# Hybrid decoder trunk: sums of squares in two rounded passes, forget columns as weights and rest in one block, second unit staged next to the scan

## What is computed

```python
def _rmsnorm(x, g, eps):
    return x * rsqrt(mean(x * x, axis=-1) + eps) * g
# mixer
u = _rmsnorm(h, mix_norm)
z = u @ w_in       # diff q/k/v | fox q/k/v | forget (8 columns) | stick q/k/v | gates
log_f = log_sigmoid(forget_logit + forget_bias)      # 8 heads
c = cumsum(log_f, axis=tokens)
# forgetting attention: logits[q, k] += c[q] - c[k]
```

## Time and profile before

| | us |
|---|---|
| time, median of 3 runs (2472.60 to 2472.94) | 2472.61 |
| the profiled execution, its own time | 2474.14 |
| its span, first to last instruction | 2472.4 |
| PE busy, share of the span | 99% |
| DVE busy, share of the span | 87% |
| ACT busy, share of the span | 60% |
| mean granted TensorE clock, share of the full 2.4 GHz | 0.998 |

### The profile page before, as it was taken

The page is one execution under the profiler, slowest core; times in us unless marked ns, Lnnn a source line. Parts: engine busy times, 40 slices in busy tenths (PEclk is TensorE's granted clock), DMA queues, the critical chain, the costliest instruction groups (busy, mean ns, idle before and its releaser), DMA issues.

```text
span 2472.4 us, 48558 instructions
## 1 busy us (share of the span) xinstructions
PE 2450.5 (99%) x15664; PEld 2220.4 (90%) x15664; DVE 2147.3 (87%) x3881; ACT 1471.4 (60%) x2882; POOL 4.4 (0%) x13
## 2 busy tenths in 40 slices
PE   8999999999999999999999999999999999999998
PEld 7999888888899889998889998888888998899987
DVE  8999868898898779998699997798898986799986
ACT  7666447777654456664466664577776554566643
POOL 0000000000000000000000000000000000000000
PEclk9999999999999999999999999999999999999999
DMA  4332332212232333233322223222212323233333
GB/s 159 113 105 102 111 103 62 68 61 61 76 104 85 96 102 103 102 106 119 108 95 102 102 94 128 86 69 67 62 60 69 103 103 102 87 111 109 102 111 103
DMA packets 65254, 235.57 MB, mean 95 GB/s; under 512 B 7232, under 2 KB 7616, under 8 KB 65088
## 3 DMA queue, kind: packets, MB, share of 16 engines
q1 hardware_dynamic: 65088, 233.51, 28.7%
HBM read 231.38 MB, written 2.10 MB: 94 GB/s over the span
## 4 chain that ended last, share of the span: by engine, by line
PE 90%; DVE 5%; ACT 2%; issue 2%; DMA 0%; DVEq 0%; SPq 0%; ACTq 0%
PE ps L657 28%; PE ps L659 28%; PE ps L658 28%; PE ps L829 1%; DVE w_lo L1721 1%; PE ps L818 1%; PE ps L872 1%; PE ps L871 1%; PE ps L820 1%; DVE area L1721 1%; DMA w_raw<-weights 0%; PE ps L885 0%; PE ps L835 0%; PE ps L886 0%; ACT w_hi L1111 0%
## 5 line engine op out<-in xcount | busy, mean ns | idle before, releaser
L1111 ACT ACTIVATE w_hi<-w_raw 128x512 fp32r<-128x512 f32 (+1 forms) x876 | 628.3, 724 | 473.2 <-PE ps L659 230.5
L1721 DVE TENSOR_TENSOR w_lo<-w_raw,w_hi 128x512 fp32r<-128x512 f32 (+1 forms) x876 | 703.0, 808 | 116.3 <-ACT w_hi L1111 100.3
L657 PE MATMUL ps<-u_hi,w_hi 128*128 128x256 f32 (+1 forms) x2432 | 790.4, 325 | 5.1 <-DVE w_lo L1721 3.3
L659 PE MATMUL ps<-u_hi,w_lo 128*128 128x256 f32 (+1 forms) x2432 | 781.9, 322 | 0.0
L658 PE MATMUL ps<-u_lo,w_hi 128*128 128x256 f32 (+1 forms) x2432 | 781.2, 321 | 0.0
L658 PE MATMUL ps<-area,w_hi 128*128 128x256 f32 (+1 forms) x1764 | 581.4, 330 | 0.0
L657 PEld LDWEIGHTS ps<-u_hi,w_hi 128*128 128x128 f32 x2432 | 463.8, 191 | 43.6 <-issue 5.2
L659 PEld LDWEIGHTS ps<-u_hi,w_lo 128*128 128x128 f32 x2432 | 463.6, 191 | 35.0
L658 PEld LDWEIGHTS ps<-u_lo,w_hi 128*128 128x128 f32 x2432 | 464.0, 191 | 33.3 <-issue 1.4
L657 PE MATMUL ps<-area,w_hi 128*128 128x256 f32 (+1 forms) x1400 | 480.5, 343 | 0.4 <-DVE h L1743 0.4
L659 PE MATMUL ps<-area,w_lo 128*128 128x256 f32 (+1 forms) x1400 | 478.1, 341 | 0.0
(11 more groups left out here) (185 smaller groups left out, 2926.1 us busy)
## 6 DMA issues: line engine op xcount, KB each, us to landing
w_raw<-weights SPq DMA_DIRECT2D x435, 512.0 KB, 3.6
h<-x SPq DMA_DIRECT2D x4, 512.0 KB, 7.8
out<-scratch_whole SPq DMA_DIRECT2D x8, 256.0 KB, 2.2
scratch_whole<-const_b SPq DMA_DIRECT2D x1, 512.0 KB, 9.7
scratch_whole<-lambdas SPq DMA_DIRECT2D x1, 256.0 KB, 2.7
scratch_whole<-const_r SPq DMA_DIRECT2D x1, 192.0 KB, 8.9
cst<-const SPq DMA_DIRECT2D x1, 137.0 KB, 7.9
par<-params SPq DMA_DIRECT2D x1, 94.0 KB, 2.4
```

Source lines behind the costliest of these rows:

```text
L657: pe.matmul(dst, hi, x_hi, start=start, stop=False, **kw)
L659: return pe.matmul(dst, lo, x_hi, start=False, stop=stop, **kw)
L1111: return act.activation(dst, src, ACT.Copy)
L1721: return dve.tensor_tensor(dst, src, hi_part.bitcast(F32), ALU.subtract)
```

## The change

Four parts.

1. `sum_of_squares` becomes two float32r passes: ACT rounds `acc` to `acc_hi` (`squares_hi`), DVE makes `acc_lo = acc - acc_hi` (`squares_lo`), and PE multiplies each by ones. The two halves lie in piece 6 of `w_hi` and `w_lo`. The last of the seven sums stays as it was. PE now waits for `acc_lo_set`.
2. Places: `squares_lo` stands in DVE's program of an FFN after `second`, in a mixer after the `lo` of the forget blocks. `squares_hi` stands on ACT in an FFN after `scaled`, in a mixer after the `hi` of the forget blocks.
3. A forget block now holds the rounded columns in its first 64 columns and their rest in the other 64, so PE does two passes instead of three. Its result has the two parts on the two halves of the partitions: ACT copies them crosswise (two copies of 64x512 from PSUM), DVE adds them and multiplies by `rstd`.
4. DVE's `take(1)` moves from behind `bias_l` to right behind the scan, and `qk_lo(2, 2, 1)` of a mixer's first tile from behind the key bias to ahead of it.

The diff, without the lists of semaphores:

```diff
-R_IDENT, R_CAUSAL, R_STRICT, ROUNDED = 0, 1, 2, 3
+R_IDENT, R_CAUSAL, R_STRICT, R_ONES, ROUNDED = 0, 1, 2, 3, 4
+IN_BF16 = R_ONES
...
+        ones_r = sb("ones_r", P, F32R)
...
+        acc_hi, acc_lo = (w[:, (PIECES - 1) * SEQ:PIECES * SEQ] for w in (w_hi, w_lo))
...
             def sum_of_squares():
+
+                c.skip(acc_set, ND)
+                pe.wait_ge(acc_lo_set, c.next(acc_lo_set))
+                pe.matmul(ps[:, 7, :], ones_r[:], acc_hi, start=True, stop=False)
+                pe.matmul(ps[:, 7, :], ones_r[:], acc_lo, start=False, stop=True).then_inc(ms_set, 1)
+
+            def last_sum_of_squares():
 
                 pe.wait_ge(acc_set, c.next(acc_set, ND))
                 pe.matmul(ps[:, 7, :], ones, acc, start=True, stop=True).then_inc(ms_set, 1)
...
                     at = PT_HI + k * P
-                    last = three(ps[:, AUX, :], area[:, at:at + P], area[:, at + ND * P:at + ND * P + P], *u(k),
-                                 start=k == 0, stop=k == ND - 1)
+                    u_k_hi, u_k_lo = u(k)
+                    pe.matmul(ps[:, AUX, :], area[:, at:at + P], u_k_hi, start=k == 0, stop=False)
+                    last = pe.matmul(ps[:, AUX, :], area[:, at:at + P], u_k_lo, start=False, stop=k == ND - 1)
...
+            def squares_hi():
+
+                act.wait_ge(acc_set, c.next(acc_set, ND))
+                hi(acc_hi, acc).then_inc(acc_hi_set, 1)
...
                 scaled(3, own + 3)
+                squares_hi()
                 across_hi(0)
...
                 for k in range(ND):
-                    dst = wf_bank[:, k * P:(k + 1) * P].rearrange("p (r n) -> p r n", n=N_FOX)
-                    last = hi(dst, wf_source(layer, k))
+                    last = hi(wf_part(k, 0), wf_source(layer, k))
                 last.then_inc(wf_hi_set, 1)
+                squares_hi()
                 norm()
                 split(0)
                 qk_hi(2, 0, 0)
+                act.wait_ge(forget_mm, layer + 1)
+                for hd in range(2):
+                    last = act.activation(tile(4)[half(hd), :], ps[half(1 - hd), AUX, :], ACT.Copy)
+                last.then_inc(forget_turned, 1)
                 act.wait_ge(forget_in, c.next(forget_in))
...
-            hi(cst_b[:], scratch[:, 0:ROUNDED * P])
+            hi(cst_b[:], scratch[:, 0:IN_BF16 * P])
+            hi(ones_r[:], scratch[:, IN_BF16 * P:ROUNDED * P])
...
+            def squares_lo():
+
+                dve.wait_ge(acc_hi_set, c.next(acc_hi_set))
+                lo(acc_lo, acc, acc_hi).then_inc(acc_lo_set, 1)
...
                 second(3, own + 7)
+                squares_lo()
                 turned_sum(0, own)
...
-                    last = lo(dst, wf_source(layer, k), hi_part)
+                    last = lo(wf_part(k, 1), wf_source(layer, k), wf_part(k, 0))
                 last.then_inc(wf_set, 1)
+                squares_lo()
                 dve.wait_ge(rstd_set, c.next(rstd_set))
...
-                dve.tensor_tensor(y, ps[:, AUX, :], rstd[:], ALU.mult).then_inc(vec_done, 1)
+                dve.wait_ge(forget_turned, layer + 1)
+                dve.tensor_tensor(y, ps[:, AUX, :], run, ALU.add).then_inc(vec_done, 1)
+                dve.wait_ge(vec_done, c.next(vec_done))
+                dve.tensor_tensor(y, y, rstd[:], ALU.mult).then_inc(vec_done, 1)
...
                 dve.tensor_tensor_scan(run, soft, neg, 0.0, ALU.add, ALU.add).then_inc(forget_in, 1)
+                take(1, 1.0)
...
-                stage(1, 1.0)
+                split(1)
+                qk_lo(2, 2, 1)
                 dve.scalar_tensor_tensor(neg, run_hi, mask(2), base_r[:], ALU.mult, ALU.add).then_inc(vec_done, 1)
...
                     qk_lo(2, 0, 0)
-                qk_lo(2, 2, 1)
+                    qk_lo(2, 2, 1)
                 take(2, 1.0)
```

More of the change, by code:

```diff
@@ L218, in trunk @@
         cst = sb("cst", C_END)
-        cst_b = sb("cst_b", ROUNDED * P, BF16)
+        cst_b = sb("cst_b", IN_BF16 * P, BF16)
+        ones_r = sb("ones_r", P, F32R)
         par = sb("par", P_END)
@@ L453, in trunk @@
         acc_set = sem("acc_set")
+        acc_hi_set = sem("acc_hi_set")
+        acc_lo_set = sem("acc_lo_set")
         u_hi_set = sem("u_hi_set")
@@ L468, in trunk @@
         forget_mm = sem("forget_mm")
+        forget_turned = sem("forget_turned")
         forget_in = sem("forget_in")
@@ L650, in _ @@
         def _(pe):
-            c = Counts(pe, [g_part_set, snap_set, w_set, u_set, acc_set, rstd_set, hid_set, g_set, h_set, wf_set, staged,
+            c = Counts(pe, [acc_lo_set, g_part_set, snap_set, w_set, u_set, acc_set, rstd_set, hid_set, g_set, h_set, wf_set, staged,
                             rows_set, qk_set, v_set, exp_set, prob_set, pt_set, o_sq, o_rstd, o_norm,
@@ L1062, in _ @@
                 pe.matmul(ps[:, 0, :], area[:, 0:P], area[:, 0:SEQ], start=True, stop=True)
-            sum_of_squares()
+            last_sum_of_squares()
         SQ = tile(5)
@@ L1070, in times @@
             return par[:, bass.ds(gain, 1)]
-        wf_bank = area[:, PT_HI:PT_HI + 2 * ND * P]
+        wf_bank = area[:, PT_HI:PT_HI + ND * P]
         def neg_max(buf, i):
@@ L1085, in wf_source, with wf_part @@
             at = P_WF + layer * (ND * N_FOX) + k * N_FOX
-            return par[:, bass.ds(at, N_FOX)].unsqueeze(1).broadcast_to([P, P // N_FOX, N_FOX])
+            return par[:, bass.ds(at, N_FOX)].unsqueeze(1).broadcast_to([P, HEAD // N_FOX, N_FOX])
+        def wf_part(k, part):
+            at = k * P + part * HEAD
+            return wf_bank[:, at:at + HEAD].rearrange("p (r n) -> p r n", n=N_FOX)
         def keys(part, j):
@@ L1105, in _ @@
         def _(act):
-            c = Counts(act, [sum_set, *landed, unit_done, act_done, h_set, ms_set, gate_in, hid_set, forget_in,
+            c = Counts(act, [acc_set, sum_set, *landed, unit_done, act_done, h_set, ms_set, gate_in, hid_set, forget_in,
                              staged, turned, score_set, max_set, probs_turned, o_mm, o_ms,
@@ L1714, in _ @@
         def _(dve):
-            c = Counts(dve, [w_hi_set, w_set, sum_set, snap_set, unit_done, vec_done, h_set, sq_set, acc_set, u_hi_set,
+            c = Counts(dve, [acc_hi_set, w_hi_set, w_set, sum_set, snap_set, unit_done, vec_done, h_set, sq_set, acc_set, u_hi_set,
                              rstd_set, gate_out, g_hi_set, qk_hi_set,
@@ L2148, in forget @@
                 for k in range(ND):
-                    dst, hi_part = (wf_bank[:, (n + k) * P:(n + k + 1) * P].rearrange("p (r n) -> p r n", n=N_FOX)
-                                    for n in (ND, 0))
-                    last = lo(dst, wf_source(layer, k), hi_part)
+                    last = lo(wf_part(k, 1), wf_source(layer, k), wf_part(k, 0))
                 last.then_inc(wf_set, 1)
+                squares_lo()
                 dve.wait_ge(rstd_set, c.next(rstd_set))
@@ L2714, in constants @@
     block(R_STRICT)[:] = np.where(q >= k, NEG, 0)
+    block(R_ONES)[:] = 1
     pos = np.arange(SEQ)
```

## The result

The changed kernel takes 2483.67 us (median of 6 runs, 2482.5 to 2484.4), the kernel before, measured beside it, 2472.78 (6 runs): slower, by a ratio of 1.0042 (95% interval 1.0032 to 1.0052).

What follows compares the result with a forecast made beforehand. PE, busy 99% of the span, was taken as the bound. First FFN +1.5, other FFNs -1.2, mixers +5.1 and clock +1.4 made +6.8 on 2472.61: 2479.4 us, range 2474.3 to 2483.5.

Steps and rivals of the forecast that it cites:

- What leaves PE: Six sums 0.41 us cheaper each (2.4), two forget products 1.8 each (3.6): 6.1 us less if nothing else moved.
- The wait in the mixers: PE idles 2.6 us at the sum for `squares_lo`, eating what sum and forget product give up: +0.06 us a mixer.
- `rstd` late and the chain behind it: In a mixer `rstd` comes 2.4 us late, the product with it 2.2, the key bias 2.9.
- The transposes: In each mixer's first tile PE waits 2.4 us for the last stick weights, plus 0.1 for filling up: +2.5.
- The first FFN: PE waits for `squares_lo`, is 3.5 us late behind the sum; slack at unit 4 absorbs part: +1.5 us.
- The other three FFNs: No wait at the sum, 0.41 us gained in each: -1.2 us.
- The clock: Falls to 1.2 GHz once, in the first FFN's 4.4 us of idleness: +1.4 us; falls in mixers only in the range.
- the forecast without the clock: Whole kernel, 1.5 - 1.2 + 5.1 = +5.4 us; as the rival of no clock fall, 2478.0 us, chance 0.22.
- No stall at the transposes: Rival: in the mixers the key bias is not late enough to stall them; 2472.9 to 2474.3 us, chance 0.12.
- Faster: Rival: `squares_lo` comes early enough in mixers and first FFN, the full 6.1 us come off; 2466.5 us, chance 0.06.
- The passes not cheaper: Rival: a sum in two float32r passes costs like one in float32, 2.4 us are added; 2481.8 us, chance 0.05.

Runs made afterwards that it cites:

- run 6: Kernel before with the forget product in two passes, new staging order and ACT's split and table load ahead of the key bias copies; sums in float32: 2469.00 us.
- run 7: As run 6, with the sums in two rounded passes only in the second, third and fourth FFN: 2467.17 us.
- run 1: Changed kernel with unread products filling PE's new waits at the first FFN's sum, the mixers' sums and the first tile's turning: 2479.36 us.
- run 5: Changed kernel with, on ACT in a mixer's first tile, the split of slot 2 and sigmoid table load ahead of the key bias copies: 2478.43 us.
- run 4: Changed kernel with the sum's rounding earlier on DVE and ACT: ahead of an FFN's half tile work and a mixer's forget columns: 2476.47 us.
- 2: Kernel before with only the sums in two rounded passes; forget product in three passes and staging order as before: 2483.21 us.
- 3: Kernel before with only the forget product in two passes and the new staging order; sums in float32: 2473.54 us.

## Why the prediction was right or wrong, by its steps

- **What leaves PE: right.** Once nothing waits, run 6 gives 4.0 us for the 3.6 of the two forget products and run 7 gives 5.8 for 4.9; the intervals reach 2.2 us either way. The trace of run 6 says where more can come from: PE gains 2.3 a mixer by the end of the forget product, 1.8 by its passes and the rest by the small stall ahead of it.
- **The wait in the mixers: right.** `squares_lo` was to end 4.85 us behind the end of the last adding of squares (359.20 to 364.05 by the old clock); after, that adding ends at 361.97 and `squares_lo` at 366.81, 4.84 later. The 8 rest columns took 1.16, 0.1 more than by the slope. By the profile's count PE idled 2.48. The +0.06 of this stage shows only in the second mixer, where the clock stayed up: 4.90 late ahead of the sum, 4.98 behind the forget product. In the first it is +1.7, of which 1.6 are the clock.
- **`rstd` late and the chain behind it: right in size.** The delay of the key bias against PE's own position at the forget product was to be 2.9. Measured: its last operation ends at 388.19 instead of 380.97, 7.2 later, while PE behind the forget product is 4.4 later: 2.8. One cover failed, though: ACT's crosswise copies were to hide behind `qk_lo`; in the first mixer the slowed forget product ended late, and DVE waited for them until 375.55. In the second mixer, at the full clock, they were hidden as forecast. The bias operation took 0.49 instead of the 0.68 of before, which took a little of it back.
- **The transposes: right.** PE's two waits there add up to 1.65 idle, and to 2.35 from start to start (forecast 2.4).
- **The first FFN: right.** The sum began 4.6 behind the last adding of squares; forecast +1.5 without the clock, and the 2.8 of lateness ahead of the mixer is that, 1.6 for the clock, less 0.3 by which this execution began sooner. The wait for unit 4 is gone, as said.
- **The other three FFNs: right.** No wait at the sum, and in the third FFN its two passes take 0.46 to the next one (1252.70 to 1253.16). Run 7 against run 6 gives 1.8 for a forecast of 1.2, which the two medians can't tell apart.
- **The clock: right in kind, wrong in count.** This is the step that failed. I took one fall, by comparing the first FFN's idle time of 4.4 us with the end of the kernel, and left the mixers' waits "in the range". The profiled run has three falls at 1.6, 1.6 and 1.5 us, and its time is the fastest of the six; the mean clock of four others is lower still. The term was 1.4; it measured 4.7 in that trace, and 4.3 by run 1 against the changed kernel (5.0, each against its own kernel before). The mixers' waits should have been in the forecast: two sums of 2.6 us and two stuttering transposes of 2.4 us are four chances, and even an even chance for each would have added two falls, 2.8 us. All else in the sum came out near its size, so the forecast without the clock, +5.4, stands against 5.9 in run 1.
- **The profiled execution of before** holds 1.0 us of its own that has nothing to do with the change. ACT waited 2.5 us for a weight transfer ahead of the third FFN, and PE idled twice early in that FFN, at 1240 us; after, that wait is 1.0 and PE doesn't idle. That the one made the other is my reading; no run tests it. PE makes up about 1.1 us against that execution there in the trace of every other kernel, whatever the edit. Comparing two single traces alone would have made the change look 1 us better than it is:

```profile
ACT w_hi L1111 <- DMA w_raw<-weights: 2.5, 1, 2.5
...
ACT w_hi L1130 <- DMA w_raw<-weights: 1.0, 1, 1.0
```

- **The rivals.** "No stall at the transposes" is what runs 5 and 6 made true, by taking work out of the chain that the rival named. "Faster" asked for `squares_lo` ahead of the two splits, and no run puts it there: run 4 moved it in the mixers only ahead of the rest columns, and run 7 is faster because it leaves the waiting sums in float32. "The passes not cheaper" falls with the 0.46 above and with run 7.

## What to carry to other kernels

When one engine is busy 99% of the span, taking passes from it pays only where the operands made in their place are ready first: before such a change, read where the other engines' queues stand at the moment the busy engine arrives, and put the new small operation ahead of the long ones there. When the busy engine leaves a stage early, the next thing it needs is the end of a chain on the others; look in that chain for work that waits behind a semaphore without needing it, as a split and a table load did here. And give every new wait on TensorE of some 2.5 us its chance of a fall of the clock in the forecast, not only the longest: of six such waits at the mixers' sums in the traces here, three brought one.

## What the runs showed of the hardware

The granted clock of TensorE fell to 1.2 GHz in the first mixer although PE had gone back to work: PE idled until 366.86, worked at 2.4 GHz for 1.5 us, and only then, at 368.4, was slowed for 3.4 us. So the slow stretch falls wholly on useful work, and a wait of 2.5 us costs up to 1.6 us more than itself. In the second mixer the same wait at the sum passed without a fall, and the turning brought one, with two idle times of 0.5 and 1.15 us and little work between them. In run 5 the first FFN was slowed for longer, from 24.7 to 31.5 us, and it cost 2.4 us there instead of 1.6:

```profile
22.00:25.00 3.00, 0.09 (x1) 0.00 (x0) 2.96 (x8) 3.00 (x9) 0.00 (x0) 0.95 0.36 142
25.00:31.00 6.00, 4.66 (x11) 3.70 (x12) 6.00 (x14) 5.30 (x10) 0.00 (x0) 0.50 0.17 33
```

Equal waits do not always bring a fall. I count the profiled executions of the kernels in which nothing fills the waits:

| PE's wait | idle, us | in | with a fall |
|---|---|---|---|
| sum of the first FFN | 4.2 to 4.3 | changed, 2, 5 | 3 of 3 |
| sum of a mixer | 2.5 to 3.0 | changed, 2, 5 | 3 of 6 |
| turning, first tile | 0.5 and 1.15 | changed, 3, 4 | 1 of 6 |
| sums and unit 4 in run 4 | 1.4 to 2.0 | 4 | 0 of 4 |

Waits of up to 1.87 us in the kernel before never brought one either. What decides it in between I did not measure.
